# Odd attention: the reciprocals of the softmax sums reach the 128 partitions by a turned, split, masked row instead of by four products with the identity

## The reference, cut to what matters

```
logits = einsum('bqhgd,bqkhd->bqhgk', q_blk, k_sel) * Dh ** -0.5
logits = where(valid, logits + bias, NEG_INF)
p = softmax(logits, axis=-1)
out = einsum('bqhgk,bqkhd->bqhgd', p, v_sel)
...
return (att * silu(gate)) @ w_out
```

## Time and profile before

| | us |
|---|---|
| median of 3 runs | 2026.94 (2026.66 to 2027.14) |
| profiled execution, whole | 2031.14 |
| its span, first to last instruction | 2029.9 |
| PE busy in the span | 1966.9 (97%) |
| DVE busy | 1435.0 (71%) |
| ACT busy | 886.9 (44%) |
| POOL busy | 659.3 (32%) |

### The profile page before, as it was taken

How to read it: one execution, slowest core, us unless ns; L and a number is a source line. 1 busy time by engine, 2 the same in 40 slices (tenths; PEclk the granted TensorE clock), 3 DMA queues, 4 the chain that set the end, 5 groups by cost and what they waited for, 6 DMA issues and landing times.

```text
span 2029.9 us, 24505 instructions
## 1 busy us (share of the span) xinstructions
PE 1966.9 (97%) x9236; PEld 1521.7 (75%) x9236; DVE 1435.0 (71%) x2172; ACT 886.9 (44%) x1589; POOL 659.3 (32%) x476
## 2 busy tenths in 40 slices
PE   8999999999999999999999999999999999999997
PEld 6778866788647777666688777888787877777885
DVE  7667768522179999355447699899998886685539
ACT  5343266333366761454312333444226764352531
POOL 3676610453201122455444000000003673235443
PEclk9999999999999999999999999999999999999999
DMA  6322340352420113211143201111133223455322
GB/s 269 124 63 81 89 158 22 111 190 89 107 64 25 50 63 99 88 63 42 54 154 124 73 33 63 52 62 54 61 114 110 87 73 125 155 195 210 106 92 104
DMA packets 72430, 197.92 MB, mean 98 GB/s; under 512 B 11182, under 2 KB 20559, under 8 KB 71800
## 3 DMA queue, kind: packets, MB, share of 16 engines
q1 hardware_dynamic: 72168, 196.35, 28.6%
q10 hardware_dynamic: 144, 0.00, 0.0%
HBM read 152.89 MB, written 46.71 MB: 98 GB/s over the span
## 4 chain that ended last, share of the span: by engine, by line
PE 56%; DVE 22%; ACT 3%; issue 2%; DMA 1%; POOL 1%; SPq 0%; DVEq 0%; ACTq 0%
PE psum L266 52%; DVE m L2953 8%; PE psum L269 3%; DVE m L2170 1%; DVE m L321 1%; DVE m L2974 1%; DMA m<-in_w 1%; POOL m L311 1%; ACT m L301 1%; DVE m L540 1%; DVE m L456 1%; DVE m L531 1%; DVE m L3152 1%; ACT m L395 1%; DVE m L3091 1%
## 5 line engine op out<-in xcount | busy, mean ns | idle before, releaser
L266 PE MATMUL psum<-m,m 128*128 128x512 f32 (+9 forms) x8436 | 1883.7, 391 | 36.0 <-DVE m L321 9.7
L266 PEld LDWEIGHTS psum<-m,m 128*128 128x128 f32 (+5 forms) x8436 | 1434.4, 186 | 455.5 <-issue 145.2
L311 POOL TENSOR_TENSOR m<-m,m 128x1024 fp32r<-128x1024 f32 (+1 forms) x122 | 309.7, 2542 | 976.0 <-ACT m L301 975.8
L301 ACT ACTIVATE m<-m 128x1024 fp32r<-128x1024 f32 (+2 forms) x166 | 173.6, 1049 | 341.5 <-PE psum L266 211.6
L2953 DVE SCALAR_TENSOR_TENSOR m<-m,m,m 128x1024 f32<-128x1024 f32 x240 | 312.4, 1303 | 6.2
L269 PE MATMUL psum<-m,m 128*128 128x128 f32 x784 | 111.9, 280 | 13.8 <-ACT m L1446 6.2
L269 PEld LDWEIGHTS psum<-m,m 128*128 128x128 f32 x784 | 91.1, 143 | 34.6 <-ACT m L1446 8.2
L2170 DVE TENSOR_SCALAR_CACHE_REDUCE m<-m,m 128x896 bf16<-128x896 f32 (+4 forms) x130 | 102.8, 848 | 1.1
L2499 POOL TENSOR_TENSOR m<-m,m 128x384 f32<-128x384 f32 (+5 forms) x48 | 72.6, 1526 | 57.6 <-DVE m L2294 45.1
L2294 DVE CUSTOM_DVE_ANT_0 m<-psum,m 128x128 f32<-128x128 f32 (+3 forms) x64 | 48.4, 756 | 39.5 <-PE psum L266 34.5
L2389 ACT ACTIVATE m<-m,m 128x1024 bf16<-128x1024 f32 (+1 forms) x62 | 64.1, 1036 | 23.2 <-DVE m L2197 23.2
(11 more groups left out here) (311 smaller groups left out, 1694.2 us busy)
## 6 DMA issues: line engine op xcount, KB each, us to landing
m<-in_w SPq DMA_DIRECT2D x164, 512.0 KB, 3.5
scr_hscr<-m SPq DMA_DIRECT2D x4, 2048.0 KB, 6.6
m<-scr_hscr SPq DMA_DIRECT2D x4, 2048.0 KB, 10.6
scr_turned<-scr_strip SPq DMA_DIRECT2D x8, 575.5 KB, 13.5
m<-in_x SPq DMA_DIRECT2D x4, 1024.0 KB, 7.9
scr_gscr<-m SPq DMA_DIRECT2D x16, 256.0 KB, 4.2
m<-in_x SPq DMA_DIRECT2D x2, 2048.0 KB, 8.5
m<-scr_turned SPq DMA_DIRECT2D x8, 512.0 KB, 4.6
```

The source lines that it names most:

```text
L266: return self.nc.tensor.matmul(out, lhsT, rhs, start=start, stop=stop, skip_group_check=True)
L301: k.nc.scalar.activation(k.hi[SLOT[i]][:, 0:kk * n], k.raw[i % 2][:, 0:kk * n], ACT.Copy).then_inc(*k.up("w_hi", i))
L311: k.nc.gpsimd.tensor_tensor(lo, raw, hi.bitcast(F32), ALU.subtract).then_inc(*k.up("w_lo", i))
```

## The change

The reciprocals of a group are split by DVE into a high part, rounded to fp32r, and a low part, the rest (both 128 x 4, 32 columns apart in a tile of 36 columns that has been cleared once). PE turns this tile by one instruction to 36 x 128. DVE multiplies it, read four times over, with a mask of 36 rows x 4 columns, which leaves row r only in the part i of the 512 columns where r = i or r = 32 + i; this goes to SBUF as fp32r. One product with a weight of ones (36 x 128) then adds high and low and gives the 512 reciprocals on each of the 128 partitions. The new PE step s3a stands one step earlier than s3 (where the unit of s1 has b = 6 or b = 2) and takes a bank of the ring for itself, so the ring gives out 16 banks per head instead of 14.

```
+    def s3a(n, Q):                                   # PE
+        bank = k.bank(O.ptb.take("recT", n, Q))
+        pe.wait_ge(*O.ptb.freed("recT", n, Q))
+        pe.wait_ge(*at("od_rec", n, Q))
+        k.tr(bank[0:36, 0:128], O.rp[Q]).then_inc(*up("od_recT_ps", n, Q))
 
     def s3(n, Q):
         bank = k.bank(O.ptb.take("rec", n, Q))
         pe.wait_ge(*O.ptb.freed("rec", n, Q))
-        pe.wait_ge(*at("od_rec", n, Q))
-        for i in range(4):
-            ins = k.mm(bank[:, 128 * i:128 * i + 128], O.recs[Q][:, i:i + 1].to_broadcast([128, 128]), k.ident, True, True)
-        ins.then_inc(*up("od_rec_ps", n, Q))
+        pe.wait_ge(*at("od_rd", n, Q))
+        k.mm(bank, O.one[0:36].to_broadcast([36, 128]), O.rd[n // 4][0:36].rearrange("p i q -> p (i q)"), True, True).then_inc(*up("od_rec_ps", n, Q))
...
             s3(O.units[i - 4][0], O.units[i - 4][1] // 4)
+        if 3 <= i < len(O.units) + 3 and O.units[i - 3][1] % 4 == 3:
+            s3a(O.units[i - 3][0], O.units[i - 3][1] // 4)
         if 2 <= i <= len(O.units) + 1:
             s2(*O.units[i - 2])
...
         if u == 18:                                  # DVE, once, ahead of the attention
             settle()
+            dve.wait_ge(*last("bits"))
+            V.memset(k.tiny[:, 0:72], 0.0).then_inc(*up("od_rclear"))
+            V.tensor_tensor(O.rmask, k.ident[:, 0:4], k.ident[:, 32:36], ALU.add).then_inc(*up("od_rmask", 0))
+            V.tensor_copy(O.one, k.ones[:, 0:1]).then_inc(*up("od_rmask"))
...
     def s1b(n, Q):                                   # DVE
         dve.wait_ge(*at("od_exp", n, 4 * Q + 3))
-        V.reciprocal(O.recs[Q], O.sums[Q]).then_inc(*up("od_rec", n, Q))
+        dve.wait_ge(*at("od_rclear"))
+        high, low = O.rp[Q][:, 0:4], O.rp[Q][:, 32:36]
+        V.reciprocal(O.recs[Q], O.sums[Q]).then_inc(*up("od_rec", n, Q, "whole"))
+        if n:
+            dve.wait_ge(*at("od_recT_ps", n - 1, Q))
+        dve.wait_ge(*last("od_rec"))
+        V.tensor_copy(high.bitcast(F32R), O.recs[Q]).then_inc(*up("od_rec", n, Q, "high"))
+        dve.wait_ge(*last("od_rec"))
+        V.tensor_tensor(low, O.recs[Q], high, ALU.subtract).then_inc(*up("od_rec", n, Q))
+
+    def s3a(n, Q):
+        bank = k.bank(O.ptb[("recT", n, Q)])[0:36, 0:128]
+        dve.wait_ge(*at("od_recT_ps", n, Q))
+        dve.wait_ge(*at("od_rmask"))
+        if (n, Q) != (0, 0):
+            dve.wait_ge(*at("od_rec_ps", *before((n, Q), 1, 2)))
+        V.tensor_tensor(O.rd[n // 4][0:36], bc(bank, 1, 4), bc(O.rmask[0:36], 2, 128), ALU.mult).then_inc(
+            *up("od_rd", n, Q, also=[("free", "od_ptb", "recT", n, Q)]))
...
             s1(*O.units[i])
+        if 3 <= i < len(O.units) + 3 and O.units[i - 3][1] % 4 == 3:
+            s3a(O.units[i - 3][0], O.units[i - 3][1] // 4)
```

More of the change, by code:

```diff
@@ L1895, in __init__ @@
         self.smr = [k.tiny[:, 128 + 8 * i:136 + 8 * i] for i in range(3)]
+        self.rp = [k.tiny[:, 36 * i:36 * i + 36] for i in range(2)]
+        self.rmask, self.one = k.tiny[:, 72:76], k.tile(k.T0 + 352, [1], F32R)
+        self.rd = [k.tile(o, [4, 128], F32R) for o in (X0 + 56 * KB, O)]
         self.sums, self.recs = ([k.tiny[:, o + 4 * i:o + 4 * i + 4] for i in range(2)] for o in (152, 160))
```

## The result

The changed kernel takes 2041.03 us (median of 4 runs, 2040.66 to 2041.35), the kernel before 2027.04 beside it (4 runs): a ratio of 1.0062, with an interval of 1.0042 to 1.0082. It is slower, and the time lies above the predicted range. The runs of one kernel lie up to 4.3 us on either side of their median, single ones 6 to 7 above it. The two profiled executions of the kernel before differ by 1.9 us in their spans and by 0.01 us inside the attention.

What follows compares the result with a forecast made beforehand. The prediction took PE to bound the kernel, busy 1966.9 of 2029.9 us. Its terms, -0.7 + 0.4 + 0.25 + 0.9 = +0.85 us on the 2026.94 median, made 2027.8, with a range of 2022.9 to 2035.2.

Steps and rivals of the forecast that it cites:

- PE's price: PE's own work per group: 0.865 us of products removed, 0.11 and 0.23 added, so 0.525 less if nothing waits.
- I take the 0.23, with 0.865 as the dear end: Price in us of the 36-row ones product on PE, taken from fp32r products in the gates; 0.865 is the fp32 price.
- Q = 1 groups, -0.10 forecast: Output product starts 0.10 us earlier per group, 0.7 for 7, as PE idles 0.4 waiting for DVE's masked product.
- Q = 0 groups, +0.05 forecast: POOL's mask holds DVE's subtraction, PE's fifth turn waits, the 0.525 is eaten: +0.05 us per group, +0.4 for 8.
- The subtraction, 0.24 us after POOL's start, has two SBUF inputs, so I let it end at 903.60: Q = 0 step on DVE: subtraction starting at 901.93 waits out POOL's mask, making the queue behind it 1.2 us late.
- The end, +0.9 forecast: Last group: masked product follows DVE's last copies with no scores to hide behind, +0.9 us, 0 as the other end.
- Once, ahead: Ahead of the attention: three small DVE instructions in the top-k pick's chain, between 0 and 0.6 us, taken as 0.25.
- The sum: Whole kernel: -0.7 + 0.4 + 0.25 + 0.9 = +0.85 us, 2027.8 on the median, called no change.
- (1): Rival: the Q = 0 subtraction gets through, each such group gives its 0.525, -3.75 us in sum, 2023.2; chance 0.15.
- a sign of being wrong: In the changed profile: subtractions of 0.17 us in all 16 groups, with a head near 20.8, would show the forecast wrong.
- (2): Rival: POOL holds the Q = 1 subtraction as well, +0.96 us for 7 groups, +8.3 in sum, 2035.2; chance 0.22.
- (3): Rival: the 36-row ones product costs 0.865 us as fp32 does, about +9 us in sum, 2037; chance 0.03.

Runs made afterwards that it cites:

- e4: Changed kernel with the ones product over all 128 rows, those behind the 36th cleared to zero; ratio 1.0039 to the kernel before.
- e9: Changed kernel with the ones product over 64 rows, rows 36 to 63 zero; one run of 2047.45 us, a time the study does not use.
- e7: The changed kernel again on another occasion, no edit; 2038.12 us against 2027.0 for the kernel before, ratio 1.0055.
- e6: As e5, but the last group has its four fp32 products again, without turn or masked product; 2022.6 us against 2027.0 before, ratio 0.9977.
- e8: The kernel before, profiled a second time without edit; 159.6 us from the first to the last product with the output gate.
- e2: As e1, with the Q = 1 turn and masked product also moved ahead of the same step's scores; ratio 1.0011 to the kernel before.
- e10: Changed kernel with the rounding copy of the reciprocals made by ScalarE, DVE's subtraction waiting for it; one run of 2046.8 us, a time not used.
- e1: Changed kernel with the Q = 0 reciprocal, copy and subtraction moved to an idle stretch of DVE; ratio 1.0024 to the kernel before.
- e5: Changed kernel with Q = 0 split early, Q = 1 turn and masked product earlier, and ones product over 128 rows; ratio 0.9988 to the kernel before.
- e3: Changed kernel with the ones and the masked rows as fp32 instead of fp32r; ratio 1.0106 to the kernel before.

## Why the prediction was wrong, point by point

**PE's price.** The failed step is "I take the 0.23, with 0.865 as the dear end". The product costs PE 0.61 in the Q = 0 groups (0.23 + 0.38, by e4) and 0.43 in the Q = 1 groups (0.23 + 0.20), 4.6 us over the 16 groups; it is the largest term of the miss that the runs place. It is not the product itself but the loads on both sides of it, which the products in the earlier trace rows, all of 128 rows, hide. That the row count decides is shown by e4 and e9; that the time lies in the loads is read from the rows of PEld. The Trainium skill (TensorE: Matmul & The Clock Gate, "Step-by-step: what each phase is for") says that a load's time goes by its columns and not by its rows, and that loads are pulled ahead of running products where the row groups do not conflict or the load goes to the background weight buffer. The first agrees with the trace, 0.18 us at 36 and 64 rows and 0.19 at 128. Of the second the runs show that it did not happen next to a load of 36 or 64 rows; why is not shown.

**Q = 1 groups, -0.10 forecast, +0.25 measured.** Right were DVE's side (the masked product starts 4.34 us after the product with the output gate, as forecast, and takes 0.68 for 0.69), the free copy and subtraction, and PE's wait (0.4 forecast, 0.38 measured). The 0.35 missing are the load of 0.20 and about 0.15 in the restart behind the wait: the weight load began 0.11 us after the masked product's end (896.82 to 896.93) and took 0.18, 0.29 in all, where I had 0.05 + 0.14 from the earlier trace rows, a turn's load that waited for a copy. The rest of 0.05 is not settled.

**Q = 0 groups, +0.05 forecast, +0.76 measured.** The mechanism was right: a small instruction between the reciprocal and the scores of b = 5 is held by POOL's mask, DVE's queue is late, and the fifth turn waits (PE waits 0.70 us, row L269 at 909.32). Of the missing 0.71, 0.38 are the loads. About 0.2 is the step "The subtraction, 0.24 us after POOL's start, has two SBUF inputs, so I let it end at 903.60", which let the copy go free: the copy is held itself (1.87 us, in all 8 groups of the first profile, in 7 of 8 of e7's), and the subtraction comes after. That was the sum which the rule of the Trainium skill (SBUF — State Buffer, "SBUF: two separate sides") gave, +1.6 us over 8 groups, and the trace agrees with the rule, not with my sentence that only two inputs count. About 0.1 is the way from the held copy of turned probabilities to the scores of b = 7 (1.06 us from start to start, where I had 0.96).

**The end, +0.9 forecast, +1.02 measured:** right, as long as the clock holds. Nine profiles have a last group that waits like this (all but before, e6 and e8). In three of them (e2, e7, e10) it fell, which cost 1.7 us in e2 and e7; in the other six it did not, nor in the three with the old end. But this is not simply a price of the change: from 829.5 to 838 us, at the attention's start, the mean granted clock is 0.80 in the first profiles of both kernels and in e1, e4, e5, e8, e9 and e10, and 1.00 in e2, e3, e6 and e7. So e2 and e7 have at the end what seven of the others have at the start (e10 has both, e3 and e6 neither): from the gates' start to the first product e7 takes 39.05 us and the changed kernel 40.76, which is 1.7 as well. What decides where it comes is not shown.

**Once, ahead:** at most 0.2, forecast 0.25.

**The sum.** 7 heads lose 1.01 instead of winning 0.05, 7.4 us; the first group, 0.6; the last, 0.1; the stray interval 0.4: 8.5 us of miss in the attention. On the spans: 10.2 us measured (2029.9 to 2040.1), 0.85 forecast, the rest being differences ahead of the attention and behind it. On the medians the miss is 13.2 (2027.8 to 2041.03), and the other 4.7 us are not found. The first series' medians stand 14.0 apart and e7's 11.1, so part of it is scatter. But scatter should go both ways, and in all eight series with several runs (the changed kernel twice, e1 to e6) the medians differ from the kernel before by 0.9 to 5.5 us more than "first to last" does. Up to 0.9 of that is the first group and the new instructions ahead; the profiles show no place for the rest, and no run looked for it.

**The rivals.** (1), the subtraction of Q = 0 gets through. By the letter it does: it takes 0.16 us in all 16 groups of the first profile, which I had written down as a sign of being wrong. But the head of 20.8 that went with it did not come, since the copy ahead takes the hold; where the copy is out of the way, the subtraction is held (1.62 in e10, 1.81 in the first group of e7). (2), the subtraction of Q = 1 held: false in the changed kernel, and 0.05 us of delay away. (3), the ones product costs 0.865: false as a mechanism (e3), though the measured 0.61 and 0.43 lie between its 0.865 and my 0.23. (Its 0.54 for Q = 1 counts from the kernel before; from the forecast it is 0.64, and the sum 2037.3.) I gave it 0.03 because the earlier trace rows spoke against it, but no row had a load of fewer than 128 rows, and I had written so myself. Its end of 2037 ought to have been in the range; with the copy's 1.6 us it would have been near 2039, and the rest to 2041 is in the part that is not found.

## What to carry to other kernels

Among products of 128 rows, one of 36 or 64 rows cost here its own weight load and the next one's, 0.2 us each; padding with zero rows, cleared once per tile, took that away. A tiny DVE instruction between SBUF tiles, a plain copy included, can wait out a whole GpSimd instruction (1.87 us here for 0.17 of work): put it where DVE is idle, and ask what is released at the same moment. And when no row shows an operation, a neighbouring row's price is one end of the range and not the forecast's certainty: 16 repetitions turned a missed 0.2 to 0.4 us into 4.6. Last, a ruler inside the attention tells causes apart far better than the whole time does, but it does not stand for the whole time: e5 gained 6.5 us by the one and 2.3 by the other.

## What the runs showed of the hardware that I had not expected

- A product of 512 columns with 36 or 64 rows: 0.48 us by its own rows and 0.61 in a row of products; with 128 rows 0.23.
- A DVE copy of 128 x 4 fp32 to fp32r between SBUF tiles, begun 0.04 us after a GpSimd instruction: 1.87 us instead of 0.17. Begun within 0.01 us of POOL's recorded start, the subtraction took 0.16 (7 groups of Q = 1); begun 0.05 behind it, 1.25. The point from which a hold applies lay between 0.00 and 0.04 us after POOL's recorded start in these places, and the one of the earlier trace rows, 0.17 late and free, does not fit this, which stays open.
- Behind an idle time of 1.35 us late in the attention PE's mean granted clock was 0.60 (e2) and 0.67 (e7) of 2.4 GHz in windows of 4.0 and 3.2 us, in some executions of a kernel and not in others, and 1.7 us went with it; in eight profiles a low stretch of that kind lay at the attention's start.
